# A routed expert layer whose experts are worked on in pairs, 128 slots beside 64, chunk by chunk

## The reference, cut to what matters

```python
D_MODEL, SEQ = 1024, 256
N_EXPERTS, TOP_K, D_FF_EXPERT = 8, 2, 3584
def swiglu(h, wg, wu, wd):
    return (jax.nn.silu(h @ wg) * (h @ wu)) @ wd

def moe_swiglu(h, w_router, wg, wu, wd):
    xt = h.reshape(-1, D)
    logits = (xt @ w_router).astype(jnp.float32)
    top_v, top_i = lax.top_k(logits, TOP_K)
    gates = jax.nn.softmax(top_v, axis=-1)
    gate = jnp.sum(jax.nn.one_hot(top_i, N_EXPERTS) * gates[..., None], axis=1)
    y = jnp.zeros_like(xt)
    for e in range(N_EXPERTS):
        y = y + gate[:, e:e + 1] * swiglu(xt, wg[e], wu[e], wd[e])
    return y.reshape(B, S, D)
```

## Time and profile before

| | us |
|---|---|
| time, median of 3 runs | 1669.54 |
| the profiled execution, first to last instruction | 1666.4 |
| TensorE busy | 1623.5 |
| VectorE busy | 1317.3 |
| ScalarE busy | 1082.2 |
| GpSimd busy | 122.1 |
| expert stage, first matmul at | 666.4 |
| each of the three full pair windows | 245.3 to 245.4 |

### The profile page before, as it was taken

The page is one execution under the profiler, slowest core; times in us unless marked ns, Lnnn a source line. Parts: engine busy times, 40 slices in busy tenths (PEclk is TensorE's granted clock), DMA queues, the critical chain, the costliest instruction groups (busy, mean ns, idle before and its releaser), DMA issues.

```text
span 1666.4 us, 20534 instructions
## 1 busy us (share of the span) xinstructions
PE 1623.5 (97%) x7691; PEld 1347.1 (81%) x7691; DVE 1317.3 (79%) x1520; ACT 1082.2 (65%) x1315; POOL 122.1 (7%) x244
## 2 busy tenths in 40 slices
PE   6999999999999996999999999999999999999996
PEld 5788888888888885888888888888888888888884
DVE  4776676575554567898998998998998998998997
ACT  4664574644443562777777777776776776777774
POOL 3433432010000101000000000000000000000000
PEclk9999999999999997999999999999999999999998
DMA  9547445446465633799999999999999999999993
GB/s 347 184 130 216 142 135 177 132 141 202 131 215 189 208 102 102 267 373 381 359 370 337 354 367 371 362 367 333 353 369 373 354 375 338 355 369 355 374 363 131
DMA packets 152928, 462.58 MB, mean 278 GB/s; under 512 B 7870, under 2 KB 12236, under 8 KB 152700
## 3 DMA queue, kind: packets, MB, share of 16 engines
q1 hardware_dynamic: 150384, 454.32, 75.5%
q0 software_dynamic: 1824, 5.11, 1.2%
q10 hardware_dynamic: 620, 1.83, 0.3%
HBM read 460.18 MB, written 1.05 MB: 277 GB/s over the span
## 4 chain that ended last, share of the span: by engine, by line
PE 93%; DVE 3%; DMA 2%; DVEq 1%; issue 1%; ACT 1%; SPq 0%; ACTq 0%
PE ps L2324 19%; PE ps L2322 19%; PE ps L2323 18%; PE ps L1840 8%; PE ps L1842 8%; PE ps L1841 8%; DMA raw_sb<-w_in 2%; PE ps L2349 1%; PE ps L2258 1%; PE ps L1886 1%; PE ps L1888 1%; PE ps L1887 1%; PE ps L1921 0%; DVE wlo_sb L1132 0%; PE ps L1865 0%
## 5 line engine op out<-in xcount | busy, mean ns | idle before, releaser
L1140 DVE TENSOR_TENSOR wlo_sb<-raw_sb,whi_sb 128x1024 fp32r<-128x1024 f32 x672 | 789.0, 1220 | 96.6 <-ACT whi_sb L818 95.5
L818 ACT ACTIVATE whi_sb<-raw_sb 128x1024 fp32r<-128x1024 f32 x672 | 674.9, 1053 | 243.3 <-PE ps L2324 243.3
L2322 PE MATMUL ps<-whi_sb,xlo_sb 128*128 128x512 f32 x896 | 351.2, 392 | 0.9 <-ACT xhi_sb L1076 0.9
L2324 PE MATMUL ps<-whi_sb,xhi_sb 128*128 128x512 f32 x896 | 349.1, 390 | 0.0
L2323 PE MATMUL ps<-wlo_sb,xhi_sb 128*128 128x512 f32 x896 | 348.9, 389 | 0.0
L1132 DVE TENSOR_TENSOR wlo_sb<-raw_sb,whi_sb 128x1024 fp32r<-128x1024 f32 (+2 forms) x198 | 230.1, 1204 | 143.0 <-ACT whi_sb L810 142.0
L810 ACT ACTIVATE whi_sb<-raw_sb 128x1024 fp32r<-128x1024 f32 (+2 forms) x198 | 192.3, 1022 | 160.4 <-PE ps L1842 131.2
L1840 PE MATMUL ps<-whi_sb,xlo_sb 128*128 128x512 f32 (+2 forms) x544 | 213.1, 392 | 4.0 <-DVE xlo_sb L1179 4.0
L1842 PE MATMUL ps<-whi_sb,xhi_sb 128*128 128x512 f32 (+2 forms) x544 | 209.0, 384 | 0.0
L1841 PE MATMUL ps<-wlo_sb,xhi_sb 128*128 128x512 f32 (+2 forms) x544 | 208.7, 384 | 0.0
L2322 PEld LDWEIGHTS ps<-whi_sb,xlo_sb 128*128 128x128 f32 x896 | 168.3, 188 | 35.3 <-issue 1.1
(11 more groups left out here) (351 smaller groups left out, 1514.4 us busy)
## 6 DMA issues: line engine op xcount, KB each, us to landing
raw_sb<-moe_wg SPq DMA_DIRECT2D x115, 1024.0 KB, 5.8
raw_sb<-moe_wu SPq DMA_DIRECT2D x112, 1024.0 KB, 6.0
raw_sb<-moe_wd SPq DMA_DIRECT2D x112, 1024.0 KB, 6.3
raw_sb<-w_in SPq DMA_DIRECT2D x40, 1024.0 KB, 5.2
raw_sb<-w_out SPq DMA_DIRECT2D x16, 1024.0 KB, 5.0
raw_sb<-ffn_wg SPq DMA_DIRECT2D x10, 1024.0 KB, 5.0
raw_sb<-ffn_wu SPq DMA_DIRECT2D x10, 1024.0 KB, 5.2
raw_sb<-ffn_wd SPq DMA_DIRECT2D x10, 1024.0 KB, 5.0
```

The source lines that it names most:

```text
L818: nc.scalar.activation(whi[i % SPLIT][:, c:c + KC // 2, :], raw[i % RAW][:, c:c + KC // 2, :], ACT.Copy).then_inc(hi_ready, 1)
L1140: op = V.tensor_tensor(wlo[i % SPLIT][:, c:c + KC // 2, :], raw[i % RAW][:, c:c + KC // 2, :], whi[i % SPLIT][:, c:c + KC // 2, :], ALU.su ...
L2322: mm(out, lo, whi[q % SPLIT][:, w, :], start=first, stop=False)
L2324: op = mm(out, hi, whi[q % SPLIT][:, w, :], start=False, stop=last)
```

## The change

The experts are sorted by their number of tokens. The four with the most, expert 0 always among them, are "heavy" and keep 128 slots; the other four are "light" and have 64. An expert with more tokens than its slots gets a further job. A pair is one heavy and one light job, and their chunks alternate (`PAIR_ORDER`); in the first pair (`FIRST_ORDER`) twelve heavy chunks come first, since the choice of the light expert is made meanwhile, and twelve light ones last.

For a light job the high parts of its 64 rows stand in columns 0 to 63 of one stationary operand and the low parts in columns 64 to 127. One matmul with `whi` and one with `wlo` give all four products, so a chunk has 8 matmuls. The upper and lower 64 rows of the sum are added by `fold`, a matmul with a constant that also transposes: for the light expert gate and value are first copied out of PSUM by ScalarE, each is folded, and silu, product and split are done on the folded 128x256 tile.

Gate and value are now worked on in seven blocks of 512 columns for both kinds, so 56 chunks of a pair are read in rows of 512 values; `wd` is read as before. The low part of an expert chunk is one instruction of 128x2048 that waits for both halves of the high part. The table of jobs with the sorting into kinds (`kinds`, `extras`, `table`) and the gates are made after the low parts of the first steps of the first pair. Constants are laid out anew, with those of the expert stage in a POOL DMA of their own. All pairs read their experts from the table. The chunks per expert, 42, and the buffers stay as they were.

The diff, cut to its core:

```diff
-    out += [Chunk("d", 0, WIDE, k0, WIDE_K, 0, k0 == 0, k0 + WIDE_K == kt) for k0 in range(0, kt, WIDE_K)]
...
+    up = [Chunk(which, p * NC, NC, k0, KC, p, k0 == 0, k0 + KC == KT)
+          for p in range(BLOCKS) for which in "gu" for k0 in range(0, KT, KC)]
     kt = D_FFE // PART
+    return up, [Chunk("d", 0, WIDE, k0, WIDE_K, 0, k0 == 0, k0 + WIDE_K == kt) for k0 in range(0, kt, WIDE_K)]
...
+LEAD = 12
+FIRST_ORDER = [0] * LEAD + [0, 1] * (len(JOB) - LEAD) + [1] * LEAD
+PAIR_ORDER = ([0, 0, 1, 1, 0, 1, 0, 1] + [0, 1] * 4 * (BLOCKS - 2) + [0, 1, 0, 0, 1, 0, 1, 1]
+              + [0, 0, 0] + [1, 0] * (len(JOB_DOWN) - 3) + [1, 1, 1])
...
+            for i, step in enumerate(FIRST.steps):
+                if i == LEAD + 1:
+                    sp.wait_ge(jobs_ready, 1)
+                    srcs[LIGHT_JOB] = expert(expert_at(1))
+                sp_chunk(sp, srcs[step.b][step.chunk.which], AT_MOE, i, step.chunk)
+            def pair(j):
+                srcs = [expert(expert_at(2 * j + b)) for b in range(2)]
...
+            pool.dma_start(con_moe[:, :], A["consts"][:, N_MIX:N_CONST]).then_inc(small_landed, 16)
...
-            nc.gpsimd.memset(yghi[:, :].bitcast(F32), 0.0)
-            nc.gpsimd.memset(yglo[:, :].bitcast(F32), 0.0)
-            nc.gpsimd.memset(backT[:, :, :, :].bitcast(F32), 0.0).then_inc(zeroed, 1)
...
         def dve_lo_moe(dve, i, l):
-            for c in range(0, KC, KC // 2):
-                dve.wait_ge(hi_ready, 2 * AT_MOE + 2 * i + (2 if c else 1) + 2 * PER * l)
-                op = V.tensor_tensor(wlo[i % SPLIT][:, c:c + KC // 2, :], raw[i % RAW][:, c:c + KC // 2, :],
-                                     whi[i % SPLIT][:, c:c + KC // 2, :], ALU.subtract)
-            op.then_inc(lo_ready, 1)
+            dve.wait_ge(hi_ready, 2 * AT_MOE + 2 * i + 2 + 2 * PER * l)
+            V.tensor_tensor(wlo[i % SPLIT][:, :, :], raw[i % RAW][:, :, :], whi[i % SPLIT][:, :, :],
+                            ALU.subtract).then_inc(lo_ready, 1)
...
+            def pair(j, plan):
+                for i in range(PER):
+                    if i in plan.value[HEAVY_JOB]:
+                        dve.wait_ge(split_used, number(AT_MOE, i + 1, PER, j))
+                        dve.wait_ge(hg_silu, done + p + 1)
+                        V.tensor_tensor(act_h[:, :], acc[:, HEAVY_JOB, 1, :], act_h[:, :], ALU.mult).then_inc(h_act, 1)
+                    dve_lo_moe(dve, i + SPLIT, j)
+                    if i in plan.after_value[HEAVY_JOB]:
+                        dve.wait_ge(h_hi, done + p + 1)
+                        V.tensor_tensor(alo2[:, p * NC:(p + 1) * NC], h_tp(p), ahi2[:, p * NC:(p + 1) * NC],
+                                        ALU.subtract).then_inc(h_lo, 1)
+                    if i in plan.product_l:
+                        dve.wait_ge(luT_ps, done + p + 1)
+                        dve.wait_ge(l_silu, done + p + 1)
+                        V.tensor_tensor(actT_l[:, :], l_tp(p)[1], actT_l[:, :], ALU.mult).then_inc(l_act, 1)
+                    if i in plan.split_l:
+                        dve.wait_ge(l_hi, done + p + 1)
+                        V.tensor_tensor(lo, l_blocks(actT_l[:, :]), hi, ALU.subtract).then_inc(l_lo, 1)
+                    if first(j):
+                        if i == 0:
+                            kinds()
+                        if i == 1:
+                            extras()
+                        if i == 2:
+                            table()
...
+            def light_step(i, chunk):
+                for c in range(chunk.k):
+                    both = alT[:, k * PART:(k + 1) * PART] if chunk.which == "d" else xhi[:, k, PART:2 * PART]
+                    for h in range(chunk.n // NC):
+                        mm(o, both, whi[i % SPLIT][:, w, :], start=first, stop=False)
+                        op = mm(o, both, wlo[i % SPLIT][:, w, :], start=False, stop=last)
+                op.then_inc(split_used, 1)
+            def fold(out, src):
+                for a in range(NC // PART):
+                    op = mm(out[:, a * LIGHT:(a + 1) * LIGHT], src[:, a * PART:(a + 1) * PART], C("fold"), start=True,
+                            stop=True)
...
+                for i, (b, chunk) in enumerate(plan.steps):
+                    (light_waits if b else heavy_waits)(chunk, j)
+                    pe.wait_ge(lo_ready, number(AT_MOE, i + 1, PER, j))
+                    (light_step if b else heavy_step)(i, chunk)
```

More of the change, by code:

```diff
@@ L183 @@
 WIDE_K = 2
-BLOCKS = 4
+BLOCKS = D_FFE // NC
 LAST = BLOCKS - 1
[L188 to L194, removed]
-    kt = D_FFE // PART
-    out += [Chunk("d", 0, WIDE, k0, WIDE_K, 0, k0 == 0, k0 + WIDE_K == kt) for k0 in range(0, kt, WIDE_K)]
-    return out, up
-JOB, JOB_UP = expert_chunks()
@@ L201 @@
[L201 to L209, removed]
+HEAVY_JOB, LIGHT_JOB = 0, 1
+ROUNDS = 4
+Step = namedtuple("Step", "b chunk")
+Plan = namedtuple("Plan", "steps gate value fold_g silu_l after_value product_l split_l y_out pick gather back scat_l scat_h")
@@ new lines, with plan_of, ends, both @@
+PAIR_ORDER = ([0, 0, 1, 1, 0, 1, 0, 1] + [0, 1] * 4 * (BLOCKS - 2) + [0, 1, 0, 0, 1, 0, 1, 1]
+              + [0, 0, 0] + [1, 0] * (len(JOB_DOWN) - 3) + [1, 1, 1])
+def plan_of(order, first):
+    steps = merged(order)
+    def ends(b, which, later=0):
+        return {i + later: s.chunk.block for i, s in enumerate(steps)
+                if s.b == b and s.chunk.which == which and s.chunk.last}
+    def both(which, later=0):
+        return tuple(ends(b, which, later) for b in (HEAVY_JOB, LIGHT_JOB))
+    up_end = max(max(ends(b, "u")) for b in (HEAVY_JOB, LIGHT_JOB))
+    y_out = {i: b for b in (HEAVY_JOB, LIGHT_JOB) for i in ends(b, "d")}
+    gather = {up_end + 4 + r: r for r in range(ROUNDS)}
+    scat_h = max(min(y_out) + 2, max(gather) + 2)
+    return Plan(steps, both("g"), both("u"), ends(LIGHT_JOB, "g", 1), ends(LIGHT_JOB, "g", 2), both("u", 1),
+                ends(LIGHT_JOB, "u", 2), ends(LIGHT_JOB, "u", 3), y_out, up_end + 1, gather, LEAD if first else 6,
+                None if first else 1, scat_h)
@@ L1117, in scalar_program @@
             with act.Fori(WRITTEN_OUT, n_pairs) as j:
-                for b in range(2):
-                    job(b, j)
+                pair(j, PAIR)
             act.wait_ge(x_final, 1)
@@ new lines, in light_step @@
+            def light_step(i, chunk):
+                out = acc[:, LIGHT_JOB]
+                for c in range(chunk.k):
+                    k = chunk.k0 + c
+                    both = alT[:, k * PART:(k + 1) * PART] if chunk.which == "d" else xhi[:, k, PART:2 * PART]
+                    first, last = chunk.first and c == 0, chunk.last and c == chunk.k - 1
+                    for h in range(chunk.n // NC):
+                        o = out[:, h if chunk.which == "d" else "gu".index(chunk.which), :]
+                        w = c * (chunk.n // NC) + h
+                        mm(o, both, whi[i % SPLIT][:, w, :], start=first, stop=False)
+                        op = mm(o, both, wlo[i % SPLIT][:, w, :], start=False, stop=last)
+                op.then_inc(split_used, 1)
@@ new lines, in heavy_waits @@
+            def heavy_waits(chunk, j):
+                done, p = BLOCKS * j, chunk.block
+                if chunk.which == "d":
+                    if chunk.first:
+                        pe.wait_ge(hg_silu, done + BLOCKS)
+                        pe.wait_ge(h_act, done + BLOCKS)
+                    if chunk.k0 * PART % NC == 0:
+                        pe.wait_ge(h_lo, done + chunk.k0 * PART // NC + 1)
+                elif chunk.first and p == 0 and not first(j):
+                    pe.wait_ge(yg_lo, 4 * j)
+                elif chunk.first and p:
+                    pe.wait_ge(hg_silu if chunk.which == "g" else h_act, done + p)
@@ L2350, in job @@
[L2350 to L2364 removed]
+                        elif not first(j):
+                            pe.wait_ge(scat_used, 2 * j + 1)
```

631 lines of the change are left out of this document (376 added, 255 removed).

## The result

The changed kernel takes **1645.2 us** (median, 1644.0 to 1646.5), the kernel before 1669.5 (1669.1 to 1670.1): ratio 0.9857, 95% interval 0.9843 to 0.9871. That is 24.3 us less where 41.4 were forecast. The profiled execution took 1646.5, the slowest of its four, and its span is 1644.7 (before 1666.4): 21.7 less.

The account below looks back on a forecast made before the run. TensorE bound the kernel by a hair, with memory late next at 376 GB/s: -44.4 + 5 - 3 - 1 + 2 = -41.4 us from 1666.4, so 1625, plus 3.1: 1628 us. Range 1580 to 1676; the forecast's own, 1605 to 1650.

Parts of the forecast that it names:

- TensorE was the bound by a hair: Expert pairs before the change: TensorE sets the pace at 245.4 us, the memory queue having only 2 or 3% idle.
- TensorE's sum, 210.5: TensorE's work per pair after the change: 192.8 matmuls, 14.0 transposes, gathers and scatters, 3.7 more for folds, in us.
- VectorE's sum, 219.5, ScalarE's, 195.4: Work per pair in us after the change: VectorE 219.5, before 222.2, at 2.61 per chunk; ScalarE 195.4, hidden.
- The hand-over: Three split buffers passing ScalarE, VectorE, TensorE: 6.8 us a round, 2.27 per chunk, hidden under VectorE's 2.61.
- The memory is late next, -44.4: Expert weight loads bind next at 376 GB/s: 234.3 us per pair for 245.4, 44.4 us less over four pairs.
- The edges, +3: Expert stage's start and end: 5 lost in first chunks, 3 given back, 1 gained at start, 2 added at end (us).
- The last 3.1, from span to median: Whole run: the median lies 3.1 us above the profiled span, and that doesn't change.
- the round is the bound, slower: Rival, chance 0.09: other work stretches the three split buffers' round to 9 us, 252 per pair, 1697 us in all.
- The ceiling is here: Rival, chance 0.13: memory gives no more than 360 GB/s, 244.7 us per pair, 1670 us in all.
- more memory: Rival, chance 0.15: the queue serves 394 GB/s once nobody holds it back, 223.6 us per pair, 1585 in all.
- token counts: Under other rivals, chance 0.03 together: an expert over its slots costs another pair, 1862 us; the reference routing keeps four.
- The clock: Under other rivals, chance 0.03 together: TensorE, idle one tenth of the time, loses its clock; gaps are 0.3 us a chunk.

Follow-up runs that it names:

- the kernel with 4 KB pieces: Changed kernel with TensorE returning split buffers in two halves, plus gate and value chunks of pairs 2 to 4 read as 1024-column rows: 1590.9 us.
- with halves: Changed kernel with TensorE returning each split buffer in two halves, so ScalarE's first copy of chunk i+3 may start after half the matmuls: 1595.0 us.

## Why the prediction was right in sign and half in size

*TensorE was the bound by a hair*: held. Its work went, and the time with it.

*TensorE's sum, 210.5*: too low by 7. The folds were priced as transposes, 0.132 each (3.7 more in all). The trace has 56 of them at about 0.25, two records each, 14 us: near the upper bound of the prediction (11 more). The sum is then some 217; the kernel with 4 KB pieces, where TensorE is the bound in the gate and value blocks, is busy for 217.9 of a pair.

*VectorE's sum, 219.5, ScalarE's, 195.4*: a little high (213.3 and 187 to 189 busy), every single duration as read. The records of one engine overlap: two subtractions back to back take 4.49, not 2 x 2.29. So "2.61 per chunk, and never less" is a little high too.

*The hand-over*: **this step failed.** The round was put at 6.8 us, 2.27 per chunk, hidden under VectorE's 2.61 "with 1.0 us per round to spare". The runs show 22.3 us for eight gate and value chunks, 2.79 each, so 8.4 us a round: 1.6 of foreign work and queueing per round, not under 1.0. The error is in adding up only the three steps' own times. A round isn't free to turn: ScalarE's gate copy stands behind the next weight copy, VectorE's product behind the next subtraction, TensorE's fold behind both. And the change lengthened the round exactly where it had no room, by letting VectorE wait for both halves. Since the round was held to be hidden, that was costed at nothing; it costs 30 us.

*The memory is late next, -44.4*: the pace was right, the cause was not. 376 GB/s was forecast and 371 to 374 came, but with a third of the bytes gone the time fell by 2 us. That pace and the pair of 238 us, the upper end of what the forecast would have taken as a sign, are luck; so is it luck that the measured time lies inside the forecast's own 1605 to 1650. The signs that decide failed: no landings of 10 us, no wait for `raw_sb`. The four pairs' steady gain is 7.4 + 7.4 + 7.3 + 9.8 = 31.9 (pair 1 counted like pair 2), 12.5 short. Once the round is loosened memory does stop the kernel, at 384 and 410 GB/s and 224.5 us a pair, 10 us below the 234.3 of the forecast. The rows of 2 KB, charged nothing, cost up to 3.5 us a pair there (by the medians of the two kernels, 4 us in three pairs). The Trainium skill, "DMA: Bandwidth & Descriptors", section "Where 436 GB/s comes from", puts a limit of about 358 GB/s per core on transfers out of main memory: pairs here ran at 393 and 396, so it doesn't hold for this one core at work. The Trainium skill, "Perfetto Trace Analysis", section "Roofline", has it better: 358 is a core's share when both cores of a memory domain work, and one active core can draw more, up to what its 16 DMA engines carry, about 435; the runs agree with that, with 412 the most over a stretch of landings.

*The edges, +3*: +10.2. The start costs 1.1 in place of giving 1. TensorE's gathers did begin 0.4 us sooner, but the clock, at 0.50 in both kernels there, came back at 664.9 us and not at 663.3, and the first expert matmul starts at 666.55 where it was 666.42; the other 1.0 is the first subtraction in one piece, which waits for both halves. The first pair is 5.9 worse than the others, where 5 - 3 = 2 were forecast:

```profile
681.90 0.42 DVE L1878 TENSOR_TENSOR gate_l_sb<-place_sb,con_moe_sb 128x256 f32<-128x256 f32 x1
...
684.48 0.17 DVE L1894 CAST jobs_sb<-jobs_f_sb 1x35 int32<-1x35 f32 x1
684.59 0.69 DVE L1935 TENSOR_TENSOR act_h_sb<-ps,act_h_sb 128x512 f32<-128x512 f32 x1
```

The table stands ahead of the first product on VectorE, TensorE waits 4.2 us for that product, and from 666 to 700 us memory brings 188 GB/s where it brought 244. The clock falls right behind that wait, as shown above. The buffers loaded ahead give none of it back, since nobody was short of data. The end costs 3.2, not 2:

```profile
1624.52 2.29 DVE L1267 TENSOR_TENSOR wlo_sb<-raw_sb,whi_sb 128x2048 fp32r<-128x2048 f32 x1 [1.70 <-ACT whi_sb L919]
1626.73 2.47 DVE L1921 SCALAR_TENSOR_TENSOR x_sb<-ps,gate_sb,x_sb 128x1024 f32<-128x1024 f32 x2
1629.37 1.29 DVE L1983 TENSOR_TENSOR yglo_sb<-ps,yghi_sb 128x512 fp32r<-128x512 f32 x2 [0.16 <-issue]
```

The heavy expert's scatter sums (2.47) now stand in front of the last `yglo`; with experts side by side both outputs fall due at the end. The rest comes behind it: TensorE has idled 7.7 us where it was 4.2, and its last eight matmuls all run at a granted clock of 0.50, where the first three of them were still at full clock. So the shortfall of 19.7 is 12.5 in the steady pairs and 7.2 at the edges.

*The last 3.1, from span to median*: 0.5. A run's time lies 1.8 above its own span throughout. The kernel before was profiled in an execution 1.3 under its median, the changed kernel in one 1.3 over; that is the 2.6 between 21.7 and 24.3.

*The rivals*: "the round is the bound, slower" had the place and the signs to look for (ScalarE waiting for TensorE, landings at 5 to 6 us), at 0.09, and the wrong price, 9 us a round and 252 a pair for 8.4 and 238 (its sum is 1696, not 1697). What it would take to be slower than before, 8.76 us, it missed by 0.4. "The ceiling is here" and "more memory" are both out for this kernel; token counts gave four pairs, as said. The clock, waved off with gaps of "0.3 us a chunk", did fall: the gaps aren't spread over the chunks but stand together at the pairs' boundaries, and the 10.2 us that this can cost at most would be half of the shortfall of 19.7. The range has an error too: 390 GB/s give 226 us a pair and 1594, not 1605.

## What to carry to other kernels

When the engine that binds gets less work, look first at the ring of buffers behind it: add up one full turn, with everything that stands queued between its steps on each engine, before asking about memory or totals. A merged instruction that waits for all of its input saves its fixed cost on one engine and lengthens the turn by what it no longer overlaps (here 0.07 us saved a chunk, 30 us lost). A rate that matches a forecast ceiling doesn't show that the ceiling binds: only a wait for a landing does, or a run with fewer bytes.

## What the hardware showed that I had not expected

Memory's pace with the queue always full depends on the piece: 380 to 388 GB/s with 2 KB rows and 403 to 412 with 4 KB rows in the kernels that wait for landings; the gate and value chunks once read as 4 KB rows came at 399 to 410, with hardly anybody waiting for them. Alone on the queue the two differ by 0.1 us in 5, but 4 to 6% remain when nothing else hides them. Six raw buffers let a phase run above that pace for a while: with halves, eight output chunks take 18.75 us (447 GB/s by consumption) for 16 chunks, about what TensorE's 80 matmuls at 0.23 take, while landings come at 403 to 412.

A few microseconds of TensorE's idling, close together, can cost more than themselves: behind five such places of the changed kernel the clock was at 0.50 for 3.4 or 6.8 us. The times of the kernel with 8 matmuls in every chunk go with it: 1603.8 and 1612.7 us at mean granted clocks of 0.979 and 0.974.
